# A hybrid layer with routed experts: the recurrent branch placed inside the last projection tiles, and the choice of experts done token tile by token tile

## The reference

```python
def mlstm_mixer(q, k, v, i_pre, f_pre, o_pre, norm_g):     # scan over chunks, per head
    cum = jnp.cumsum(lft, axis=-1)
    dmat = cum[..., :, None] - cum[..., None, :] + it[..., None, :]      # causal
    m_t = jnp.maximum(m_inter, jnp.max(dmat, axis=-1))
    w = jnp.exp(dmat - m_t[..., None]) * jnp.einsum('bhtd,bhsd->bhts', qt, kt)
    num = inter[..., None] * (qt @ c_mat) + w @ vt
    den = inter * (qt @ n_vec) + jnp.sum(w, axis=-1)
    h_t = num / jnp.maximum(jnp.abs(den), jnp.exp(-m_t))[..., None]
...
def hier_moe(h, gw, gb, ew, eb, w1, w3, w2):
    g_sel = jnp.argmax(g_logits, axis=-1)                 # 1 of 4 groups
    top_v, top_i = lax.top_k(e_in_group, 2)               # 2 of its 8 experts
    gate = jax.nn.softmax(top_v, axis=-1) * g_gate
    counts = jnp.bincount(eid, length=N_EXPERTS)          # rows of each expert, in blocks
    dest = starts_pad[se] + (jnp.arange(n_assign) - starts[se])
    row_tok = jnp.zeros((n_rows,), jnp.int32).at[dest].set(tok[order])
    out = jnp.zeros((t, d)).at[row_tok].add(ys * row_w[:, None])
```

## Time and profile before

| | us |
|---|---|
| median of 3 runs | 1983.13 (1977.72 to 1983.3) |
| profiled execution, its own time | 1980.05 |
| its span, first to last instruction | 1977.9 |
| mean granted TensorE clock | 0.936 |

### The profile page before, as it was taken

One profiled execution on the slowest core, in us unless ns is written; L12 is line 12 of the kernel. 1 busy time (PEld: TensorE's weight loads), 2 busy tenths in 40 slices (PEclk: granted clock), 3 DMA queues, 4 the chain that ended last, 5 costly groups with the idle time before them and its releaser, 6 DMA issues. The chain is left out here.

```text
span 1977.9 us, 24003 instructions
## 1 busy us (share of the span) xinstructions
PE 1792.6 (91%) x8818; PEld 1385.6 (70%) x8818; DVE 1407.6 (71%) x1881; ACT 908.9 (46%) x1143; POOL 223.7 (11%) x164
## 2 busy tenths in 40 slices
PE   7999999598999999999998879937999999999980
PEld 7778888486777777777776767735777777777760
DVE  5678689779888888622225662266999999999966
ACT  6543111102334434433345441005787777877752
POOL 1000000103000012000001320001211222112103
PEclk9999999658999999999999989957999999999995
DMA  4111132001343322222314751065999999999947
GB/s 185 59 43 54 56 105 71 21 1 43 96 156 124 120 88 63 81 101 60 119 33 148 265 186 43 33 265 190 387 395 398 398 404 398 396 394 395 405 160 274
DMA packets 75643, 356.64 MB, mean 180 GB/s; under 512 B 8521, under 2 KB 11081, under 8 KB 49193
## 3 DMA queue, kind: packets, MB, share of 16 engines
q1 hardware_dynamic: 66088, 321.97, 43.7%
q0 software_dynamic: 5888, 20.97, 3.3%
q10 hardware_dynamic: 3584, 12.58, 1.6%
HBM read 299.53 MB, written 55.97 MB: 180 GB/s over the span
## 5 line engine op out<-in xcount | busy, mean ns | idle before, releaser
L2156 DVE TENSOR_TENSOR wa_lo<-wa,w_hi 128x2048 fp32r<-128x2048 f32 x128 | 289.8, 2286 | 15.4 <-ACT w_hi L2069 14.1
L2069 ACT ACTIVATE w_hi<-wa 128x2048 fp32r<-128x2048 f32 x128 | 244.6, 1915 | 63.0 <-PE psum L2014 36.4
L1335 PE MATMUL psum<-h_hi,w_hi 128*128 128x512 f32 x512 | 224.7, 439 | 2.5 <-ACT gate_out L979 1.6
L1335 PE MATMUL psum<-h_hi,w_lo 128*128 128x512 f32 x512 | 203.1, 397 | 0.0
L1335 PE MATMUL psum<-h_lo,w_hi 128*128 128x512 f32 x512 | 201.7, 394 | 0.0
L167 DVE MAX8 top<-sel 128x8 f32<-128x384 f32 (+5 forms) x192 | 171.3, 892 | 4.6
L1998 PE MATMUL psum<-w_hi,xT_hi 128*96 128x512 f32 x512 | 164.7, 403 | 5.1 <-DVE wa_lo L2156 5.1
L2163 DVE TENSOR_TENSOR wb_lo<-wd,w_hi 128x2048 fp32r<-128x2048 f32 x64 | 143.9, 2288 | 34.7 <-ACT w_hi L2078 34.7
L165 DVE MATCH_REPLACE8 sel<-top,sel 128x384 f32<-128x384 f32 (+5 forms) x192 | 168.1, 875 | 0.0
L1998 PE MATMUL psum<-w_hi,xT_lo 128*96 128x512 f32 x512 | 160.6, 394 | 0.0
L1998 PE MATMUL psum<-wa_lo,xT_hi 128*96 128x512 f32 x512 | 160.5, 395 | 0.0
(11 more groups left out here) (360 smaller groups left out, 3500.8 us busy)
## 6 DMA issues: line engine op xcount, KB each, us to landing
wa<-expert_up SPq DMA_DIRECT2D x128, 1024.0 KB, 11.4
wd<-expert_down SPq DMA_DIRECT2D x64, 1024.0 KB, 11.7
w<-w_gate SPq DMA_DIRECT2D x32, 512.0 KB, 4.2
gate_pre<-gate_out SPq DMA_DIRECT2D x64, 256.0 KB, 3.7
gate<-gate_pre SPq DMA_DIRECT2D x32, 512.0 KB, 5.0
ys<-yo ACTq DMA_DIRECT2D x32, 384.0 KB, 7.0
w<-w_T SPq DMA_DIRECT2D x18, 512.0 KB, 3.8
ys<-zeros SPq DMA_DIRECT2D x7, 1152.0 KB, 5.9
```

Source lines behind the costliest of these rows:

```text
L1335: ins = nc.tensor.matmul(psum[:, 7, :], w[:, k, :], x[:, k, half * 512:(half + 1) * 512], start=(n == 0), stop=(n == BURST - 1))
L2069: nc.scalar.activation(hi_a(j, q).rearrange("p c m n -> p (c m n)"), wa[j][q][:, :, :, :].rearrange("p c m n -> p (c m n)"), ACT.Copy).the ...
L2156: nc.vector.tensor_tensor(wa_lo[j][q][:, :, :, :].rearrange("p c m n -> p (c m n)"), wa[j][q][:, :, :, :].rearrange("p c m n -> p (c m n)" ...
```

## The change

Mixer B moves from attend into project. TensorE runs its parts between the slices of tiles 6 to 15: `b_part(i, p)` is called ahead of slices 1, 4, 7, 10 and 13 of a tile's 16 (and 15 in tile 7). Tile 6 has the ends and the turned keys, tile 7 the seven state steps, tiles 8 to 15 one token block each; the norm of the last block comes beside tile 16. Banks 0 to 3, free there, take its results, one bank for each kind. To find room, `tile_buf` has two buffers instead of four. The small loads and GpSimd's gain product come early in project. VectorE splits one tile ahead instead of two, takes 3 half steps in tiles 6 and 7 together and seven in tiles 8 to 16 (four in 17), and two in each unit of A. The split of gate tile NTT + 1 moves to unit 0 of attend.

In route each token tile has psum bank 6 or 7 for its logits, and VectorE makes the choice for tile t - 1 behind the norm of tile t. The loops over nine thresholds become one wide comparison and one reduction. The one-hot tables are made in wide operations, eight at a time, and TensorE multiplies them in two runs of eight. The instructions for the overflow blocks come behind the table of tokens, and the wait for the stored rows comes ahead of the one-hot tables.

```diff
@@ project
-    tile_buf = [sb(f"tile_buf{i}", [P, SEQ], 139.25 + 4 * i) for i in range(4)]
+    tile_buf = [sb(f"tile_buf{i}", [P, SEQ], 139.25 + 4 * i) for i in range(2)]
+    B_AT = T_QC + 2
@@ project, gpsimd
+            pool.wait_ge(loads_in, 48)
+            pool.wait_ge(o_ready, 1)
+            for t in range(NT):
+                ins = pool.tensor_tensor(s.oB[:, t, :], s.oB[:, t, :], s.gainB[:, :], ALU.mult)
...
+            for b in range(NT):
+                pool.wait_ge(b_exp, b + 1)
+                pool.affine_select(out=e, in_=e, compare_op=ALU.is_ge, fill=0.0, ...).then_inc(b_masked, 1)
@@ project, scalar
-                s.split_high(act, i + 2)
+                if i + 1 < NTT:
+                    s.split_high(act, i + 2)
...
+            for n in range(NT // 2):
+                act.wait_ge(prep_ready, n + 2)
+                nc.scalar.activation(kt[...], psum[:, n % 2, :], ACT.Copy).then_inc(prep_taken, 1)
...
             for i in range(T_QC, NTT):
+                b = i - B_AT
+                if 0 <= b < NT:
+                    act.wait_ge(b_arg, b + 2)
+                    nc.scalar.activation(ex[b % 2][:, :, :], ex[b % 2][:, :, :], ACT.Exp).then_inc(b_exp, 1)
                 tile_out(i)
@@ project, vector
             s.select(link, 34)
-            for i in range(T_QC, NTT):
-                s.split_low(dve, i + 2)
-                s.select(link, 10)
...
+            s.select(link, 3)
+            dve.wait_ge(prep_taken, NT // 2 + 1)
+            nc.vector.tensor_tensor(vw[...], s.vB[...], decay[...], ALU.mult).then_inc(state_ready, 1)
+            s.split_low(dve, T_QC + 2)
+            for b in range(NT - 1):
+                dve.wait_ge(step_ready, b + 1)
...
+            for i in range(B_AT, NTT):
+                b = i - B_AT
+                if 0 < b <= NT:
+                    b_norm(b - 1)
+                if b < NT:
+                    b_exponent(b)
+                s.split_low(dve, i + 1)
+                s.select(link, 4)
+                if b < NT:
+                    dve.wait_ge(b_scores, 3 * b + 3)
+                    dve.wait_ge(b_masked, b + 1)
+                    if b >= 2:
+                        dve.wait_ge(b_pv, b - 1)
+                    nc.vector.scalar_tensor_tensor(out=wts[b % 2]..., in0=psum[:, 1, :], ...).then_inc(b_weights, 1)
+                s.select(link, 3 if i + 1 < NTT else 0)
@@ project, tensor
+            def b_part(i, p):
+                b = i - B_AT
+                if i == T_QC:
+                    if p == 0:
+                        b_ends()
+                    elif p <= NT // 2:
+                        b_keys(p - 1)
+                elif i == T_QC + 1:
+                    if 2 <= p < 5:
+                        b_step(2 * p - 4)
+                        b_step(2 * p - 3)
+                    elif p == 5:
+                        b_step(6)
+                elif 0 <= b < NT:
+                    if p == 0:
+                        b_exponents(b)
+                        b_score(b, 0)
+                    elif p == 1:
+                        b_score(b, 1)
+                    elif p < 4 and b:
+                        b_off(b, p - 2)
+                    elif p == 4:
+                        b_own(b)
...
                 for h in range(2):
                     for k in range(KC):
+                        at = h * KC + k - 1
+                        if i >= T_QC and at >= 0 and at % 3 == 0 and at <= 12:
+                            b_part(i, at // 3)
+                        if i == T_QC + 1 and at == 14:
+                            b_part(i, 5)
@@ attend: mixer B's lists of all engines and its loads are gone
+    high_at[0], low_at[0] = NTT + 1, NTT + 1
...
-                if u < 2 * NB:
-                    s.select(link, 3 if u < NB else 2)
-                elif u == 2 * NB:
-                    s.select(link, 2 * NT * TOPK)
+                s.select(link, 3 if u < NB else 2)
@@ route, vector
+            def choose(t):
+                dve.wait_ge(logits_ready, t + 1)
+                nc.vector.tensor_tensor(lg[:, t, :], psum[:, 6 + t % 2, 0:NG + NE], rb[:, :], ALU.add).then_inc(lg_taken, 1)
...
+                first_max(hot[:, 0, t, :], e1[:, :], col(3), NE, col(1))
+                link(nc.vector.scalar_tensor_tensor(out=e1[:, :], in0=hot[:, 0, t, :], scalar=-2e30, in1=e1[:, :], ...))
+                first_max(hot[:, 1, t, :], e1[:, :], col(4), NE, col(1))
...
+            for t in range(NT):
+                norm(t)
+                if t:
+                    choose(t - 1)
+            choose(NT - 1)
...
-            link(nc.vector.tensor_scalar(cnt[:, 1, :], cnt[:, 0, :], float(CAP), None, ALU.is_gt))
-            for k in range(2, MORE + 1):
-                link(nc.vector.scalar_tensor_tensor(out=cnt[:, 1, :], in0=cnt[:, 0, :], scalar=float(CAP * k), ...))
+            link(nc.vector.tensor_tensor(many[:, :, :], cnt[:, 0, :]..., steps_of[:, :]..., ALU.is_gt))
+            link(nc.vector.tensor_reduce(out=cnt[:, 1, :], in_=many[:, :, :], axis=AX.X, op=ALU.add))
...
-            for q in range(2 * NT):
-                if q >= 2:
-                    dve.wait_ge(hot_used, q - 1)
-                nc.vector.tensor_scalar(hot_c[q % 2][:, :], iota_c[:, :], asg[:, 4, q:q + 1], None, ALU.is_equal)
-                nc.vector.tensor_scalar(hot_b[q % 2][:, :], iota_b[:, :], asg[:, 5, q:q + 1],
-                                        tok_id[:, q % NT:q % NT + 1], ALU.is_equal, ALU.mult).then_inc(hot_ready, 1)
+            for k in range(2):
+                mine = slice(k * NT, (k + 1) * NT)
+                nc.vector.tensor_tensor(hot_c[:, mine, :], iota_c..., line(4)[:, mine]..., ALU.is_equal)
+                link(nc.vector.tensor_tensor(hot_b[:, mine, :], iota_b..., line(5)[:, mine]..., ALU.is_equal))
+                nc.vector.tensor_tensor(hot_b[:, mine, :], hot_b[:, mine, :], tok_id..., ALU.mult).then_inc(hot_ready, 1)
...
+            dve.wait_ge(hot_used, 1)
+            link(nc.vector.tensor_copy(s.tok_of[:, :], psum[0:CAP, 5, 0:NBLK]))
             ends = cnt[0:1, 3, :].unsqueeze(1).to_broadcast([1, N_OV, NE])
             link(nc.vector.tensor_tensor(cmpj[:, :, :], iota_j[:, :, :], ends, ALU.is_ge))
```

More of the change, by code:

```diff
@@ L185, in build @@
         s.sem = late_sem = sem
-        fresh = [sem(f"fresh{i}") for i in range(40)]
+        fresh = [sem(f"fresh{i}") for i in range(44)]
         nc.clear_and_free_semaphores(early)
@@ L1665, in _, with norm @@
             dve.wait_ge(gain_in, 16)
-            for t in range(NT):
+            def norm(t):
                 dve.wait_ge(out_ready, t + 1)
```

576 lines of the change are left out of this document (285 added, 291 removed).

## The result

The median went from 1983.22 us (4 runs, 1977.72 to 1985.42) to 1932.54 us (4 runs, 1931.20 to 1933.49): ratio 0.9751, 95% interval 0.9739 to 0.9764. The forecast was 1919 us in a range of 1904 to 1936. The profiled execution took 1933.49 us with a span of 1931.7 us, 46.2 us under the span before; the forecast was 61.3 us. The median is inside the range, and in the profiled execution a quarter of the forecast gain is missing. The two traces say where.

A forecast was written before the change was run, and what follows sets the result against it. Time could be won only where TensorE idles or crawls: the idle stretch, the low-clock recurrence, the routing. Recurrence part 49.4 + routing 11.9 + selection steps 0 = 61.3 us off 1980.05: 1919 us, range 1904 to 1936.

The forecast's parts named there:

- idle stretch: TensorE idle 17.94 us between projection and recurrence, 354.6 to 372.5 us; some 16 us of it to be won.
- the price of the records: The recurrence's 308 small matmul records in the projection tiles: 0.115 us each at the high clock, 35.4 us.
- recurrence in tiles 6 to 15: Time the recurrence adds to the projection tiles: records 35.4 us plus 47 switches at 4 to 5, sum 40 us.
- end of the block: After the last projection tile: ScalarE's copy 1.0 us and the change of blocks 0.55 us, 1.6 us before score(0).
- first unit of D: First attention unit: the moved gate-tile split delays its first transpose; 4.5 us lost, between 0 and 7.
- selection steps in C and A: 66 of 384 VectorE selection steps taken later, into the last attention part, fit there: 0 us, +2 to -2.
- routing: Choice of experts after the last token tile's logits: ends at 1326.8 instead of 1338.74 us, 11.9 us saved.
- The switch: After small matmuls the next projection matmul takes 0.31 instead of 0.23 us; 47 such parts, 4 to 5 us.
- rival (b): Small records cost 0.10 us, switches nothing, the late first attention unit nothing: 1905 us; chance 0.12.
- The cover in the tiles: VectorE makes a tile's weights at 10.4 to 11.1 us, TensorE needs them at 12.0: cover 1 us.
- rival (a): VectorE late in tiles 8 to 15, TensorE waiting about 2 us in each: 1935 us; chance 0.16.
- rival (c): Small matmuls between projection matmuls leave TensorE at the low clock in tiles 6 to 15: 2048 us; chance 0.04.

The follow-up runs named there:

- two_heads: Changed kernel with the query-state product of two heads in one 128-row matmul on a state with zeros where heads cross; ratio 0.9726 to the kernel before.
- norm_clear: Changed kernel with no selection steps in units that normalise a token tile's output and four in the unit after, in attention parts two and three; 1922.50 us.
- three_parts: Changed kernel with the recurrence's small matmuls in three places of a tile instead of five; ratio 0.9801 to the kernel before.
- pool_pieces: Changed kernel with two of GpSimd's large head-norm products cut into eight instructions each; ratio 0.9731 to the kernel before.
- best_full: Changed kernel with the edits of norm_clear, two_heads and pool_pieces, and the recurrence's other matmuls on 128 rows as well; 1905.32 us.

## Why the prediction was right, and what it missed

The side, the range and the main mechanism (idle stretch gone, recurrence at the high clock, routing passed on whole) were right; the point was 13.5 us off. Two terms were wrong, the price of the records and the moved selection steps. Step by step, in the profiled execution:

| step | forecast | measured | difference to the forecast gain |
|---|---|---|---|
| start of the kernel | 0 | 1.1 later | -1.1 (chance) |
| recurrence in tiles 6 to 15 | 40 | 48.8 | -8.8 |
| end of the block | 1.6 | 1.3 | +0.3 |
| first unit of D | 4.5 lost | 3.1 lost, 0.7 won back | +2.1 |
| later units of D, first of C | 0 | 0.8 won | +0.8 |
| selection steps in C and A | 0 (-2 to +2) | 10.0 lost | -10.0 (some 1.6 of it chance) |
| routing | 11.9 | 13.7 | +1.8 |
| sum (of rounded terms) | 61.3 | 46.5 | -14.9 |

**The records.** I priced the recurrence at 0.115 us a record, between 0.10 for the attention's products with the values and 0.14 for the exponents. For these two kinds both ends were right: the values take 0.101 here and the exponents 0.136. The others have 64 rows and cost 0.145 to 0.16 each, in groups of four. As a mean of all that a record costs, 0.115 was too low; the 0.11 inside a group is the same for all of them, and what I left out are the ends of the groups with fewer than 128 rows. The switch I read from its way out alone, 0.08, rounded to 0.10. The way in costs 0.09 more wherever the first small matmul has 4 or 64 rows, and nothing where it has 128; two_heads shows both. Seven tiles lost 1.2 us each to this, and rival (b), the cheap records, had it backwards. I could have read it: the kernel before has 64-row records at the high clock,

```profile
900.89 0.40 PE L1335 MATMUL psum<-h_hi,w_lo 128*128 128x512 f32 x1
901.21 0.70 PE L1301 MATMUL psum<-k,q 64*128 64x256 f32 x4
```

and the first starts 0.32 us after the projection matmul, not 0.23. Just behind the 1.1 us of exponents that I did use, at 380.35 us, its scores start in the same short stretch at the high clock.

**The selection steps.** This is the one step that failed by its reasoning. I compared sums: VectorE busy for 23.19 of 100 us there, two steps of 1.3 us in 4 to 7 us. The sum fits, as norm_clear shows with the same work. I did not ask what stands behind the step on VectorE's queue: the normalisation, which TensorE's next accumulation waits for. It has to be asked where a change adds a wait, and a moved step is such a case. The part before, which I took as the proof that it fits, is none. In the kernel before the steps stood ahead of five of its eight normalisations. Ahead of the first three TensorE waited for nothing, ahead of the fourth (at 803.9 us) 0.6 us and ahead of the fifth 1.2 us:

```profile
827.29 1.21 DVE L165 MATCH_REPLACE8 sel<-top,sel 128x1024 f32<-128x1024 f32 x1
```

(the normalisation follows at 828.75). Then the steps ran out, at 845 us. So that part already showed the wait, growing towards its end, and the change put steps in front of the other three and of six in the next part. The steps had 1024 columns there too, so their width is not what made the moved ones dear.

**The cover in the tiles** was as thin as counted, but held: the trace shows no wait of TensorE between 224 and 404 us, and rival (a) has no place. **The clock** stayed at 1.00 in the tiles, and rival (c) did not come, though three_parts shows that the low clock can follow small records and that the changed kernel stands one grouping away from it. The Trainium skill ("TensorE: Matmul & The Clock Gate", section "Why this matters for your kernels") asks for a TensorE kept busy; in three_parts it is busy for 4.00 of 4.00 us and the clock is at 0.57. In the 4 us before, from 301.7, it was busy for 3.94. The trace disagrees again, as in the earlier trace rows. **The first unit** lost 3.1 us, near the forecast by luck. The first transpose came 10.8 us after the first score and not 9.9; the split was slower than counted (2.97 us beside GpSimd's square, not 1.23) and the rest faster. But the clock, which I let fall behind the wait (the stretch from 480 us in the earlier trace rows that I took it from begins before its gap ends, at 481.56), fell ahead of it: it was at 0.50 from 407.9 to 414.7 us, so the twelve gate matmuls ran at the slow pace as before, the wait was 2.25 us instead of about 4, and behind it the clock was 1.00.

**The routing** went as worked out. From logits to totals 4.9 us (5.1 forecast), counting 2.5 (2.5), from there to the tables 6.9 (7.0), a half of the tables 2.0 (2.25), the overflow instructions 2.4 (2.4). Only TensorE's run over the tables was cheaper: 32 records in 5.36 us, 0.17 each, where I had taken 0.22. The sentence that it is passed on whole holds, and the condition on it ("unless the end falls before 1326 us") turned out to be the next limit: the block ends at 1292.2 us and the queues are free at 1293.6.

## What to carry to other kernels

When a step moves on an in-order engine, list what stands behind it in that queue and who waits for that; free time in the sum says nothing about it, and moving the step by one unit was worth 9 us here. Price small matmuls by the group too, and read both of its ends: here a record of 65 to 130 columns cost 0.11 us whatever its rows, and a group with fewer than 128 rows some 0.3 us on top, so zeros that fill 64 rows up to 128 can pay. And when small matmuls go between large ones, try them spread first: the same records in fewer, longer groups cost 10 us here.

## What the hardware showed that I had not expected

- Four float32 records of 64 rows and 65 columns cost 0.78 us between 512-column matmuls; two of 128 rows and 130 columns for the same product cost 0.22. Eight records of 128 columns cost 1.18 us with 4 rows and 0.88 with 128. Inside a group all of these start 0.11 us apart; the difference lies in the first and the last record and on the way in.
- Sixteen small records in a row, 2.5 us with TensorE busy for all but 0.06 us, left the clock at 0.57 over the next 4 us in four of eight tiles and at 1.00 in the other four; twelve in 1.7 to 1.9 us left it at 1.00 in all.
- A one-column VectorE instruction lasted 3.66 us beside one GpSimd instruction of 3.62 us, and 0.65 beside eight pieces of it.
- Behind the sixteen transposes of the first output the clock fell in two_heads (0.52 over 494 to 498 us), pool_pieces (0.66), three_parts and best_full, and stayed at 1.00 in the changed kernel and the seven others that have the recurrence in the tiles. Which of them it hits was not settled.
